# A two-block transformer kernel: expert weight loads moved and divided, residual products and a gather put elsewhere

## The chip, the cores and the metric

One core of a Trainium2 chip (trn2) runs the kernel. The metric is the device time of one execution in microseconds (us). Before the change, three runs took 1562.51, 1562.71 and 1564.31 us; the median is 1562.71. DMA rates are in GB/s, sizes of transfers in KB of the profile (2048 KB = 2.10 MB).

## The reference

Two blocks over 256 tokens of width 1024, float32 throughout. The second block ends in a mixer product and a mixture of experts, and only these two are touched:

```python
def second_block(x, ...):
    h = h + mixer_block(rmsnorm(h, norm1_g[l]), ...)   # ends in merged @ w_o
    h = h + hier_moe(rmsnorm(h, norm2_g[l]), w_group[l], w_router[l], w1[l], w3[l], w2[l])

def mixer_block(...):
    merged = sigmoid(gc) * y_conv + sigmoid(ga) * y_attn    # gc, ga = u @ w_in parts
    return merged @ w_o                                     # y_attn = attention @ w_attn_out

def hier_moe(u, ...):   # group by argmax, then the best 2 of its 8 experts
    # every expert e: (silu(x @ w1[e]) * (x @ w3[e])) @ w2[e], weighted, added to its tokens
```

There are 64 experts with an inner width of 512: w1, w3 and w2 are 2.10 MB each for an expert, 403 MB together, and each is read once from HBM.

## The kernel before, in words

**Engines and memory.** The five engines run programs written out by hand; semaphores order them. SyncE (SP) issues all weight loads, in one fixed order, each behind a wait for the semaphore which says that the place is free. While SP waits, everything behind it in that order waits too. The weights live in `arena`, 11 places of 2.10 MB (128 partitions x 4096 floats).

**The dense part.** Weight units ("wao0" is the first half of w_attn_out, "wo1" the second half of w_o) go through a ring of four places; TensorE adds 1 to `dense_used` for each unit that it is done with, and `static_units` waits for that count. The last four products are `seven(0)` to `seven(3)`, matrix products of 256 x 1024 x 1024 done as seven half-size products each with sums of operands made by VectorE (DVE), in the order 5, 1, 6, 7, 2, 3, 4 (line 1505); seven(2) is for ga, seven(3) for w_attn_out with the units wao0 and wao1. DVE reads these two units first for a difference of weights (line 2436). Then comes `wo(half, n)`, merged @ w_o for one half of the tokens (128) and one half of the columns (line 1557): eight matmuls 128x512 over the eight chunks of 128 rows. It reads the transposed merged rows from `mrg` (in arena place 8).

**Between the blocks' last product and the experts.** For each half of the tokens: DVE adds the product to `h_res` (line 2619), GpSimd (POOL) copies the result to `h` in another order of columns (line 793), ACT takes squares, TensorE turns h_res (`turn_h`, line 1565) and makes the router's product (`logits`, line 1577). DVE routes (lines 2632 to 2644), TensorE counts ranks (lines 1600, 1678, 1681 to 1683), DVE makes the selection matrix `sel` for the first two experts (line 2660). `gather_first(half)` (line 1618) multiplies h by sel: chunk c of 128 columns, 64 token places; ACT scales chunks 0 to 3 (line 3074), DVE chunks 4 to 7. Two products of the identity with the rows of the residual (lines 1679 and 1684 for token half 0, 1728 for half 1) put the residual into PSUM banks 0 to 3, to which every expert's result is added.

**The experts.** They are taken in 32 pairs. `MOE_SLOTS` numbers the places of arena; a pair has six units of 2.10 MB: k = 0 to 3 for w1 and w3, k = 4 and 5 for w2. Even pairs use one set of places, odd pairs another; place 0 serves both. Pair 0's w1 and w3 are loaded in quarters: arena places 0, 1 and 2 (`load_quarter`, lines 662 and 665; 4 x 512 KB and 4 x 1024 KB; they only wait for `attn2_done`, the end of the attention), then place 4. `first_up` (line 1700) is pair 0's up product: chunk by chunk c, four matmuls each; behind chunks 0, 1, 3 and 5 it adds 1 to `quarter_used`, by which SP loads pair 1's half pieces of place 0 (lines 729 and 731) and pair 2's first places (line 684). `first_rows` and `xg_ready` say that the gathered rows are there. All later pairs run `expert_up` (line 1630), `scatter` (1661), `gather_pair` (1610), `turn_pair` (1637, 1641), `expert_down` (1652). Place 5 (pair 0's k = 4) is free when half of pair 0's down product is done (`down_half`).

**Pair 1 before the change.** Its k = 1 goes to arena place 9 (free with wo0), k = 2 to place 10 (free with wo1), k = 4 to place 8 (mrg and others; free with wo1), k = 5 to place 3 (h_res and others; free when squares, POOL's copies and the residual products of token half 0 are done, `res_taken`). k = 4 and 5 are loaded in halves (`load_part`, line 715). The order on SP's queue is:

```python
for k in (0, 1, 2, 4, 5, 3) if pair in (1, 2) else range(UNITS_PAIR):
    if (pair, k) == (1, 1):
        load_part(4, 1)
        load_part(5, 0)
```

Of the kernel before, what the change touches and what calls it, by code (L numbers as in the profile page):

```python
# [233 lines left out]
def two_blocks(nc, t, out):  # L234

    with ExitStack() as ctx:
# [155 lines left out]
        mrg = xn2.rearrange("p a b -> p (a b)").rearrange("p (c s) -> p c s", c=KC)  # L392
# [63 lines left out]
        def moe_count(slot, turn):  # L456

            return 16 * turn + ((48 if turn == 1 else 64) if slot == 0 else 16 if slot in (1, 2, 3, 9, 10) else 0)
# [104 lines left out]
        quarter_used, res_taken = sem("quarter_used"), sem("res_taken")  # L563
# [56 lines left out]
        def _(sp):  # L620
# [32 lines left out]
            static_units(UNIT["downC"], len(UNITS))  # L653
# [33 lines left out]
            def moe_wait(pair, k):  # L687
# [24 lines left out]
            def load_part(k, part):  # L712

                at = moe_slot(1, k)
                sp.dma_start(MOE_SLOTS[at][:, part * 2048:(part + 1) * 2048], t["w2"][k - 2, :, part * 2048:(part + 1) * 2048]
                             ).then_inc(moe_loaded[at], 16)

            for pair in range(PAIRS):
                for k in (0, 1, 2, 4, 5, 3) if pair in (1, 2) else range(UNITS_PAIR):
                    if (pair, k) == (1, 1):  # L720
                        load_part(4, 1)
                        load_part(5, 0)
                    if pair == 1 and k in (4, 5):
                        moe_wait(pair, k)
                        load_part(k, k - 4)
                        continue
                    if (pair, k) == (1, 3):
# [3 lines left out]
                        sp.dma_start(MOE_SLOTS[0][:, 2048:4096], t["w3"][3, :, 2048:4096]).then_inc(moe_loaded[0], 16)  # L731
                        continue
# [68 lines left out]
        def _(pe):  # L801
# [745 lines left out]
            def wo(half, n):  # L1547
# [4 lines left out]
                for c in range(KC):  # L1552
                    if not n and c in (0, 4):
                        pe.wait_ge(mrg_ready, M_ORDER.index((half, c // 4)) + 1)
                    if not half and not n and c == 1:
                        release_seven(3)
                    last = mm(ps[:, BANKS[step][n], :], mrg[:, c, half * P:(half + 1) * P], slot_view(u)[:, c, :],  # L1557
                              start=(c == 0), stop=(c == KC - 1))
                last.then_inc(bank_filled, 1)
# [8 lines left out]
            def logits(half, n):  # L1568
# [7 lines left out]
                for c in range(4 * n, 4 * n + 4):  # L1576
# [20 lines left out]
            logits(1, 0)  # L1597
            turn_h(1, 1, (4, 3))
            pe.wait_ge(assigned, 1)
# [15 lines left out]
            def gather_first(half):  # L1615

                for c in range(KC):
# [4 lines left out]
                if half:  # L1622
# [1509 lines left out]
```

## Time and profile before

| | |
|---|---|
| median of 3 runs | 1562.71 us (1562.51 to 1564.31) |
| profiled execution | 1561.92 us, its span 1560.1 us |
| TensorE matmul busy | 1263.3 us (81% of the span) |
| DVE, ACT, POOL busy | 516.9, 228.8, 17.8 us |
| DMA | 501.40 MB, 321 GB/s over the span |
| chain that ended last | PE 58%, DMA 39%, DVE 1% |
| up products of the looped pairs (L1630) | 276.9 us busy, 255.4 us idle before, for DMA |

The span is cut into 40 slices of 39 us on the page: TensorE is full (9 tenths) in the first 19 and at 5 to 7 tenths in the rest; the DMA engines are at 9 tenths from about the same place on. Times of busy engines are not the kernel's time: what counts is which wait ends last in each stage. PE is TensorE, PEld its weight loads, SPq the queue of SyncE. A float32 matmul shows as two records. Lines (L1630) are those of the kernel before.

### The profile page before, as it was taken

The numbers are of one execution on the slowest core, as the hardware profiler recorded it, in microseconds if no ns is written. First come the engines' busy times: TensorE is split into PE (matmuls) and PEld (weight loads), VectorE is DVE, ScalarE is ACT, GpSimd is POOL, SyncE is SP. The second block draws the span as 40 slices with busy tenths as digits, with TensorE's granted clock in tenths as the row PEclk, the third lists the DMA queues.
The fourth block names the chain that finished last, engine by engine and source line by source line (L and its number), as shares of the span: only waits on it lengthen the run. The fifth ranks groups of instructions, "written<-read, shape, count | busy, mean of one in ns | idle before, by whom it ended". The sixth has DMA issues, their size and how long they took to land.

```text
span 1560.1 us, 16698 instructions
## 1 busy us (share of the span) xinstructions
PE 1263.3 (81%) x6953; PEld 642.1 (41%) x6953; DVE 516.9 (33%) x1096; ACT 228.8 (15%) x649; POOL 17.8 (1%) x30
## 2 busy tenths in 40 slices
PE   9999999999999999997676576577576576476577
PEld 4665644444588544543232232223233223223223
DVE  6554577785453674311011111111111111111101
ACT  2435213111122101211001001001001001001001
POOL 2000000000000000100000000000000000000000
PEclk9999999999999999999788888788888789788889
DMA  9531756405433449899999999999999999999997
GB/s 302 210 114 55 245 155 205 155 35 216 157 113 109 166 157 370 347 429 428 428 429 428 429 427 430 427 428 428 429 428 428 428 428 429 427 428 429 429 426 323
DMA packets 93419, 501.40 MB, mean 321 GB/s; under 512 B 6797, under 2 KB 34817, under 8 KB 68160
## 3 DMA queue, kind: packets, MB, share of 16 engines
q1 hardware_dynamic: 92608, 500.00, 78.9%
q0 software_dynamic: 768, 0.85, 0.3%
q8 instruction: 25, 0.41, 0.1%
q14 instruction: 18, 0.15, 0.0%
HBM read 499.78 MB, written 1.05 MB: 321 GB/s over the span
## 4 chain that ended last, share of the span: by engine, by line
PE 58%; DMA 39%; DVE 1%; issue 0%; SPq 0%; ACT 0%; DVEq 0%
DMA arena<-in_w 38%; PE ps L1630 17%; PE ps L1253 8%; PE ps L862 7%; PE ps L1505 6%; PE ps L1305 3%; PE ps L857 2%; PE ps L1067 2%; PE ps L1557 2%; PE ps L907 2%; PE ps L1437 2%; PE ps L1207 1%; DMA arena<-in_w_in 1%; PE ps L1375 1%; PE ps L1280 1%
## 5 line engine op out<-in xcount | busy, mean ns | idle before, releaser
L1630 PE MATMUL ps<-arena,hT 128*32 128x512 f32 x1984 | 276.9, 721 | 255.4 <-DMA arena<-in_w 255.4
L1630 PEld LDWEIGHTS ps<-arena,hT 128*32 128x32 f32 x1984 | 69.2, 130 | 462.6 <-issue 319.8
L2722 DVE TENSOR_TENSOR moe_hid<-moe_hid,ps 64x512 f32<-64x512 f32 x32 | 22.1, 690 | 482.8 <-ACT moe_hid L3090 482.8
L1652 PE MATMUL ps<-arena,moe_turned 128*32 128x512 f32 x1024 | 116.7, 595 | 28.0 <-DVE moe_turned L2724 27.8
L1610 PEld LDWEIGHTS ps<-sel,h 128*128 128x128 f32 x992 | 113.2, 192 | 24.1 <-issue 24.1
L1610 PE MATMUL ps<-sel,h 128*128 128x64 f32 x992 | 117.2, 276 | 0.0
L3090 ACT ACTIVATE moe_hid<-ps 64x512 f32<-64x512 f32 x32 | 18.8, 588 | 656.2 <-PE ps L1630 650.5
L862 PE MATMUL ps<-hT,arena 128*128 128x256 f32 x512 | 113.9, 380 | 0.1
L862 PEld LDWEIGHTS ps<-hT,arena 128*128 128x128 f32 x512 | 96.8, 190 | 15.0 <-issue 2.2
L3074 ACT ACTIVATE hT<-ps,gcol 128x64 f32<-128x64 f32 x252 | 55.0, 328 | 158.5 <-PE ps L1610 156.8
L1505 PE MATMUL ps<-arena 128*128 128x512 f32 x176 | 77.3, 593 | 0.0
L2724 DVE COPY moe_turned<-ps 128x512 f32<-128x512 f32 x32 | 22.1, 692 | 161.8 <-PE ps L1641 161.8
L1253 PE MATMUL ps<-arena 128*128 128x512 f32 x160 | 71.0, 592 | 0.0
L1652 PEld LDWEIGHTS ps<-arena,moe_turned 128*32 128x32 f32 x1024 | 32.7, 109 | 87.3 <-issue 70.6
L1661 PE MATMUL ps<-moe_y,moe_turned 64*128 64x512 f32 x256 | 63.6, 615 | 0.8 <-DVE moe_y L2726 0.8
L2726 DVE COPY moe_y<-ps 128x512 f32<-128x512 f32 x32 | 22.1, 691 | 123.4 <-PE ps L1652 123.4
L1253 PE MATMUL ps<-arena,hT 128*128 128x512 f32 x120 | 53.3, 592 | 0.0
L1505 PEld LDWEIGHTS ps<-arena 128*128 128x128 f32 x176 | 33.2, 190 | 41.1 <-issue 38.7
L1253 PEld LDWEIGHTS ps<-arena 128*128 128x128 f32 x160 | 29.8, 190 | 34.4 <-issue 34.2
L1305 PE MATMUL ps<-arena 128*128 128x512 f32 x96 | 42.6, 593 | 0.0
L1661 PEld LDWEIGHTS ps<-moe_y,moe_turned 64*128 64x128 f32 x256 | 22.0, 186 | 42.8 <-issue 41.1
L2177 DVE SCALAR_TENSOR_TENSOR arena<-ps,arena 128x255 f32<-128x255 f32 (+1 forms) x88 | 35.7, 472 | 6.9 <-ACT arena L2931 6.9
(465 smaller groups left out, 1245.4 us busy)
## 6 DMA issues: line engine op xcount, KB each, us to landing
arena<-in_w SPq DMA_DIRECT2D x184, 2048.0 KB, 29.3
arena<-in_w_in SPq DMA_DIRECT2D x18, 2048.0 KB, 8.5
arena<-in_w_up SPq DMA_DIRECT2D x22, 1024.0 KB, 9.4
arena<-in_w SPq DMA_DIRECT2D x14, 1024.0 KB, 13.2
arena<-in_w_down SPq DMA_DIRECT2D x5, 2048.0 KB, 13.7
arena<-in_w_out SPq DMA_DIRECT2D x2, 2048.0 KB, 14.3
arena<-in_w_conv_out SPq DMA_DIRECT2D x2, 2048.0 KB, 7.8
arena<-in_w_attn_out SPq DMA_DIRECT2D x2, 2048.0 KB, 7.8
```

Source lines behind the costliest of these rows:

```text
L857: last = mm(ps[:, at, :], xT[:, c, bank * P:(bank + 1) * P], w[:, c, :], start=(c == 0), stop=(c == KC - 1))
L862: last = mm(o, w[:, c, q * P:(q + 1) * P], xT[:, c, :], start=(c == 0), stop=(c == KC - 1))
L907: last = mm(ps[:, BANK1[product], :], lhs[:, c, :], rhs[:, c, :], start=(c == 0 and product != 3), stop=(c == 3), skip_group_check=True)
L1253: last = mm(up_seven_bank(m, product), lhs, rhs, start=(c == 0 and product not in (2, 3)), stop=(c == 3), skip_group_check=True)
L1305: return mm(ps[:, bank, :], x, w, start=(i == 0), stop=(i == NPAIR - 1))
L1505: last = mm(bank7(g, product), lhs, rhs, start=(c == 0 and product not in (2, 3)), stop=(c == 3), skip_group_check=True)
L1610: last = mm(ps[:, GT, c * 2 * CAP:(c + 1) * 2 * CAP], hview[:, half, c, :], sel[:, half, :], start=(half == 0), stop=(half == 1))
L1630: last = mm(ps[k * CAP:(k + 1) * CAP, UP, :], x[:, c, (k % 2) * CAP:(k % 2 + 1) * CAP], w[:, at:at + DE], start=(c == 0), stop=(c == KC - 1))
L1652: last = mm(ps[k * CAP:(k + 1) * CAP, DN, :], a[:, m * 64 + (k % 2) * CAP:m * 64 + (k % 2 + 1) * CAP], w[:, at:at + 512], start=(m == 0), ...
L1661: last = mm(ps[:, 2 * half + n, :], sT[rows, half * P:(half + 1) * P], moe_y[rows, :], start=False, stop=False, skip_group_check=True)
L2177: v.scalar_tensor_tensor(yy, u[:, 0:S - 2 + tap], prm[:, 0, c + 44 * tap:c + 44 * tap + 1], yy, ALU.mult, ALU.add).then_inc(ffn_chain if t ...
L3074: return a_(xg[:, c, :], ps[:, bank, c * 2 * CAP:(c + 1) * 2 * CAP], ACT.Copy, scale=gcol[:, 3, c:c + 1])
```

## The change

1. **Order of loads.** The eight quarter transfers into arena places 0, 1 and 2 are issued before wao0, wao1, wo0 and wo1 instead of behind them.
2. **Places given up in pieces.** The layout of `mrg` puts token half 0 into the first quarter of place 8's columns, token half 1 into the next; the first quarter is loaded (w2 of pair 1, k = 4, columns 0 to 1024) when wo(0, 1) is done, the second when wo(1, 1) is. wo(1, 1) adds 1 to `dense_used` behind its chunk 3, and the first half of place 10 is loaded then; the release at its end is one higher.
3. **Residual products.** All four (both token halves) stand behind first_up, before pair 1's gather, and read `h` (rows with a step of eight elements); `res_taken` is gone, and place 3 waits for `h_turned` instead.
4. **Router product.** logits(1, 0) is cut: chunks 0 and 1 before turn_h(1, 1), chunks 2 and 3 behind it.
5. **First gather.** Of token half 1, chunks 0 to 5 are gathered before first_up, chunks 6 and 7 between its chunks 1 and 2.

```diff
-        mrg = xn2.rearrange("p a b -> p (a b)").rearrange("p (c s) -> p c s", c=KC)
+        mrg = xn2.rearrange("p h (c s) -> p h c s", c=KC)
...
-            return 16 * turn + ((48 if turn == 1 else 64) if slot == 0 else 16 if slot in (1, 2, 3, 9, 10) else 0)
+            return 16 * turn + ((48 if turn == 1 else 64) if slot == 0 else 32 if slot == 9 else 16 if slot in (1, 2, 3, 8, 10) else 0)
...
-            static_units(UNIT["downC"], len(UNITS))
+            static_units(UNIT["downC"], UNIT["wao0"])
...
                     sp.wait_ge(rms_ready, 8)
                     sp.wait_ge(h_moved, 4)
-                    sp.wait_ge(res_taken, 1)
+                    sp.wait_ge(h_turned, 4)
                 else:
-                    sp.wait_ge(dense_used, released(UNIT[{3: "wao0", 4: "wao1", 7: "wo0", 8: "wo1", 9: "wo1"}[at]]))
+                    sp.wait_ge(dense_used, released(UNIT[{3: "wao0", 4: "wao1", 7: "wo0", 8: "wo1", 9: "wo1"}[at]]) + (at >= 8))
...
+            for k in range(3):
+                moe_wait(0, k)
+                load_quarter(MOE_SLOTS[k], k)
+            static_units(UNIT["wao0"], len(UNITS))
             for pair in range(PAIRS):
-                for k in (0, 1, 2, 4, 5, 3) if pair in (1, 2) else range(UNITS_PAIR):
+                for k in (0, 1, 2, 4, 5, 3) if pair in (1, 2) else range(0 if pair else 3, UNITS_PAIR):
                     if (pair, k) == (1, 1):
-                        load_part(4, 1)
-                        load_part(5, 0)
+                        load_part(4, 2048, 4096)
+                        load_part(5, 0, 2048)
+                        sp.wait_ge(bank_filled, filled(PROD["wo_h0"], 1))
+                        load_part(4, 0, 1024)
                     if pair == 1 and k in (4, 5):
                         moe_wait(pair, k)
-                        load_part(k, k - 4)
+                        load_part(k, *((1024, 2048), (2048, 4096))[k - 4])
                         continue
...
+                    if (pair, k) == (1, 2):
+                        at = moe_slot(1, 2)
+                        sp.wait_ge(dense_used, released(UNIT["wo1"]))
+                        sp.dma_start(MOE_SLOTS[at][:, 0:2048], t["w3"][2, :, 0:2048]).then_inc(moe_loaded[at], 16)
+                        moe_wait(1, 2)
+                        sp.dma_start(MOE_SLOTS[at][:, 2048:4096], t["w3"][2, :, 2048:4096]).then_inc(moe_loaded[at], 16)
                         continue
...
+                    if half and n and c == 3:
+                        last.then_inc(dense_used, 1)
...
-            logits(1, 0)
+            logits(1, 0, (0, 1))
             turn_h(1, 1, (4, 3))
+            logits(1, 0, (2, 3))
...
+            def take_residual(half, n):
+
+                rows = h[:, half, :].rearrange("p (c n) -> p n c", c=KC)[:, n * 64:(n + 1) * 64, :]
+                mm(ps[:, 2 * half + n, :], ident, rows, start=True, stop=False, skip_group_check=True)
...
-            mm(ps[:, 0, :], ident, h_res[:, 0, 0:512], start=True, stop=False, skip_group_check=True)
...
-            mm(ps[:, 1, :], ident, h_res[:, 0, 512:1024], start=True, stop=False, skip_group_check=True).then_inc(res_taken, 1)
             pe.wait_ge(sel_ready, 2)
             pe.wait_ge(h_moved, 4)
-            gather_first(1)
+            gather_first(1, range(0, 6))
             def first_up():
 
                 for c in range(KC):
+                    if c == 2:
+                        gather_first(1, (6, 7))
...
-                    for n in range(2):
-                        rows = h[:, 1, :].rearrange("p (c n) -> p n c", c=KC)[:, n * 64:(n + 1) * 64, :]
-                        mm(ps[:, 2 + n, :], ident, rows, start=True, stop=False, skip_group_check=True)
+                    for half in range(2):
+                        for n in range(2):
+                            take_residual(half, n)
```

How the instructions stand now. On SP's queue, before the dense part's last loads (in_w_attn_out_2 is wao, in_w_o_2 is wo, w1, w3 and w2 are expert weights; - is before, + is the change):

```order
 L633 DMA arena<-in_w_in_2 128x8x512 [waits dense_used] x2
-L633 DMA arena<-in_w_attn_out_2 128x8x512 [waits dense_used] x2
-L633 DMA arena<-in_w_o_2 128x8x512 [waits dense_used] x2
 L662 DMA arena<-in_w1_2 128x2x512 [waits attn2_done]
 L662 DMA arena<-in_w1_2 128x2x512
```

The four loads of wao and wo have moved down past the eight quarter transfers of places 0, 1 and 2, and now stand before those of place 4.

On the same queue, the loads of pair 1, from k = 0 to the first of pair 2:

```order
 L684 DMA arena<-in_w1_2 128x4096 [waits m_turned]
 L715 DMA arena<-in_w2_2 128x2048 x2
+L715 DMA arena<-in_w2_2 128x1024 [waits bank_filled]
 L684 DMA arena<-in_w1_2 128x4096 [waits dense_used]
-L684 DMA arena<-in_w3_2 128x4096 [waits dense_used]
-L715 DMA arena<-in_w2_2 128x2048 [waits dense_used]
-L715 DMA arena<-in_w2_2 128x2048 [waits res_taken,h_moved,rms_ready]
-L729 DMA arena<-in_w3_2 128x2048 [waits quarter_used]
-L731 DMA arena<-in_w3_2 128x2048 [waits quarter_used]
+L741 DMA arena<-in_w3_2 128x2048 [waits dense_used]
+L743 DMA arena<-in_w3_2 128x2048 [waits dense_used]
+L715 DMA arena<-in_w2_2 128x1024 [waits dense_used]
```

One transfer of 4096 columns has become two of 2048, and one of 2048 two of 1024, of which the first stands ahead of place 9's load; the rest keeps its order.

On TensorE, from the first token half's gather to first_up's third chunk, before:

```order
L1618 MATMUL ps<-sel,h 128x64 x7
L1678 MATMUL ps<-moe_turned,consts 128x64
L1679 MATMUL ps<-arena,consts 128x512
L1681 MATMUL ps<-moe_turned,consts 128x64 [waits assigned]
L1682 MATMUL ps<-moe_turned,consts 128x64
L1683 MATMUL ps<-moe_turned,consts 128x64
L1684 MATMUL ps<-arena,consts 128x512
L1618 MATMUL ps<-sel,h 128x64 [waits h_moved,sel_ready]
L1618 MATMUL ps<-sel,h 128x64 x7
L1700 MATMUL ps<-arena,hT 32x512 [waits moe_loaded0,first_rows]
```

and with the change, up to the two chunks inside first_up:

```order
L1698 MATMUL ps<-moe_turned,consts 128x64
L1700 MATMUL ps<-moe_turned,consts 128x64 [waits assigned]
L1701 MATMUL ps<-moe_turned,consts 128x64
L1702 MATMUL ps<-moe_turned,consts 128x64
L1638 MATMUL ps<-sel,h 128x64 [waits h_moved,sel_ready]
L1638 MATMUL ps<-sel,h 128x64 x5
L1720 MATMUL ps<-arena,hT 32x512 [waits moe_loaded0,first_rows]
L1720 MATMUL ps<-arena,hT 32x512 x3
L1720 MATMUL ps<-arena,hT 32x512 [waits first_rows]
L1720 MATMUL ps<-arena,hT 32x512 x3
L1638 MATMUL ps<-sel,h 128x64 x2
```

The two residual products (128x512) are gone from here, and two of the gather's eight matmuls stand behind eight of first_up's; a row further down, `L1728 MATMUL ps<-h,consts 128x512 x2` has become `L1633 MATMUL ps<-h,consts 128x512 x4`.

## Rows read from the trace of the kernel before

**Rows 1.** Page, parts 2 and 4: rate by slice, and the chain by line

```profile
GB/s 302 210 114 55 245 155 205 155 35 216 157 113 109 166 157 370 347 429 428 428 429 428 429 427 430 427 428 428 429 428 428 428 428 429 427 428 429 429 426 323
...
DMA arena<-in_w 38%; PE ps L1630 17%; PE ps L1253 8%; PE ps L862 7%; PE ps L1505 6%; PE ps L1305 3%; PE ps L857 2%; PE ps L1067 2%; PE ps L1557 2%; PE ps L907 2%; PE ps L1437 2%; PE ps L1207 1%; DMA arena<-in_w_in 1%; PE ps L1375 1%; PE ps L1280 1%
```

**Rows 2.** Chain of work, 540 to 700 us: start us, us, what

```profile
631.61 0.44 PE ps L1565 x4
...
641.85 6.88 PE ps L1557 x16
...
648.87 1.08 PE ps L1577 x8
...
656.10 0.91 PE ps L1684 x2
657.02 1.73 PE ps L1618 x16
658.75 7.00 PE ps L1700 x64
665.75 3.63 PE ps L1728 x4
...
685.10 12.72 DMA arena<-in_w
```

**Rows 3.** Windows: busy us (x) of PE, PEld, DVE, ACT, POOL, then PEclk, DMA share, GB/s

```profile
552.00:561.00 9.00, 9.00 (x22) 3.99 (x21) 8.48 (x10) 0.00 (x0) 0.00 (x0) 1.00 0.00 0
593.00:616.00 23.00, 23.00 (x61) 10.35 (x60) 12.68 (x14) 1.96 (x4) 0.00 (x0) 1.00 1.02 391
641.00:650.00 9.00, 8.85 (x34) 4.70 (x34) 3.36 (x15) 1.12 (x2) 0.49 (x1) 1.00 0.72 258
657.00:662.00 5.00, 5.00 (x49) 2.68 (x51) 2.60 (x13) 2.21 (x5) 0.00 (x0) 1.00 0.97 338
```

**Rows 4.** SP's queue, timeline 555 to 760 us: start, us, engine, line, operation

```profile
561.04 7.24 SPq L633 DMA_DIRECT2D arena<-in_w_attn_out  x2
...
592.36 3.40 SPq L662 DMA_DIRECT2D arena<-in_w  x4
```

**Rows 5.** Single transfers by line: issue duration ns, issue time, then us to landing

```profile
L633 SPq DMA_DIRECT2D arena<-in_w_in x1: 546/546/546, 543.9 to 543.9; - x1
...
DMA to landing us min/median/max: 7.9/7.9/7.9
...
L715 SPq DMA_DIRECT2D arena<-in_w x1: 328/328/328, 657.1 to 657.1; - x1
...
DMA to landing us min/median/max: 5.1/5.1/5.1
...
L729 SPq DMA_DIRECT2D arena<-in_w x1: 328/328/328, 659.8 to 659.8; - x1
...
DMA to landing us min/median/max: 5.8/5.8/5.8
...
L684 SPq DMA_DIRECT2D arena<-in_w x1: 328/328/328, 676.5 to 676.5; - x1
...
DMA to landing us min/median/max: 11.5/11.5/11.5
```

**Rows 6.** Timeline of DVE and PE, 579 to 590 us: DVE's sum for wao, PE's product

```profile
579.52 2.29 DVE L2436 TENSOR_TENSOR arena<-arena 128x2048 f32<-128x2048 f32 x1
...
584.79 3.60 PE L1505 MATMUL ps<-arena 128*128 128x512 f32 x8
```

**Rows 7.** Timeline, 631 to 662 us, in brackets idle time and releaser

```profile
649.51 1.09 POOL L793 COPY h<-arena 128x512 f32<-128x512 f32 x1 [8.72 <-DVE arena L2619]
...
655.22 0.43 PE L1681 MATMUL ps<-moe_turned,consts 128*128 128x64 f32 x2 [0.27 <-DVE moe_turned L2644]
...
656.59 2.02 PEld L1618 LDWEIGHTS ps<-sel,h 128*128 128x128 f32 x16 [0.41 <-DVE sel L2660]
...
657.89 0.93 ACT L3074 ACTIVATE hT<-ps,gcol 128x64 f32<-128x64 f32 x4 [1.78 <-PE ps L1618]
```

More of the change, by code:

```diff
@@ L562, in two_blocks @@
         piece_in = sem("piece_in")
-        quarter_used, res_taken = sem("quarter_used"), sem("res_taken")
+        quarter_used = sem("quarter_used")
         SEL_FIRST, SCATTERED_FIRST = PAIRS + 1, PAIRS + 1
@@ L706, in moe_wait, with load_part @@
                     sp.wait_ge(h_moved, 4)
[L707 removed]
+                    sp.wait_ge(h_turned, 4)
                 else:
[L709 to L712 removed]
+                    sp.wait_ge(dense_used, released(UNIT[{3: "wao0", 4: "wao1", 7: "wo0", 8: "wo1", 9: "wo1"}[at]]) + (at >= 8))
+            def load_part(k, lo, hi):
                 at = moe_slot(1, k)
[L715 to L716 removed]
+                sp.dma_start(MOE_SLOTS[at][:, lo:hi], t["w2"][k - 2, :, lo:hi]).then_inc(moe_loaded[at], 16)
+            for k in range(3):
+                moe_wait(0, k)
+                load_quarter(MOE_SLOTS[k], k)
+            static_units(UNIT["wao0"], len(UNITS))
             for pair in range(PAIRS):
[L719 removed]
+                for k in (0, 1, 2, 4, 5, 3) if pair in (1, 2) else range(0 if pair else 3, UNITS_PAIR):
                     if (pair, k) == (1, 1):
[L721 to L722 removed]
+                        load_part(4, 2048, 4096)
+                        load_part(5, 0, 2048)
+                        sp.wait_ge(bank_filled, filled(PROD["wo_h0"], 1))
+                        load_part(4, 0, 1024)
                     if pair == 1 and k in (4, 5):
                         moe_wait(pair, k)
[L725 removed]
+                        load_part(k, *((1024, 2048), (2048, 4096))[k - 4])
                         continue
@@ L1556, in wo @@
                         release_seven(3)
-                    last = mm(ps[:, BANKS[step][n], :], mrg[:, c, half * P:(half + 1) * P], slot_view(u)[:, c, :],
+                    last = mm(ps[:, BANKS[step][n], :], mrg[:, half, c, :], slot_view(u)[:, c, :],
                               start=(c == 0), stop=(c == KC - 1))
+                    if half and n and c == 3:
+                        last.then_inc(dense_used, 1)
                 last.then_inc(bank_filled, 1)
@@ L1566, in turn_h, with logits @@
                 last.then_inc(h_turned, 1)
-            def logits(half, n):
+            def logits(half, n, chunks=range(4)):
                 if n:
@@ L1575, in logits @@
                     pe.wait_ge(hT_act, 21 + half)
-                for c in range(4 * n, 4 * n + 4):
+                for c in (4 * n + k for k in chunks):
                     last = mm(ps[:, 6 - half, 0:NG + NE], hT[:, c, half * P:(half + 1) * P], router_w[:, c, :],
@@ L1612, in gather_pair, with gather_first @@
                 last.then_inc(gathered, 1)
-            def gather_first(half):
-                for c in range(KC):
+            def take_residual(half, n):
+                rows = h[:, half, :].rearrange("p (c n) -> p n c", c=KC)[:, n * 64:(n + 1) * 64, :]
+                mm(ps[:, 2 * half + n, :], ident, rows, start=True, stop=False, skip_group_check=True)
+            def gather_first(half, chunks=range(KC)):
+                for c in chunks:
                     last = mm(ps[:, 2 + c // 4, (c % 4) * 2 * CAP:(c % 4 + 1) * 2 * CAP], hview[:, half, c, :], sel[:, half, :],
@@ L1621, in gather_first @@
                         last.then_inc(first_rows, 1)
-                if half:
+                if half and KC - 1 in chunks:
                     last.then_inc(gathered, 1)
@@ L3043, in _ @@
                 act.wait_ge(m_turned, k + 1)
-                a_(mrg[:, 4 * n:4 * n + 4, half * P:(half + 1) * P], ps[:, bank, :].rearrange("p (c s) -> p c s", c=4),
+                a_(mrg[:, half, 4 * n:4 * n + 4, :], ps[:, bank, :].rearrange("p (c s) -> p c s", c=4),
                    ACT.Copy).then_inc(mrg_ready, 1)
```

1 line of the change is left out of this document (added).

## The prediction

> **What bounds the kernel now.** I read the page's second and fourth parts first. From slice 18 of 40 (39 us each, so from 663 us) the DMA rate stands at 426 to 430 GB/s up to the last slice, and 38% of the chain that ended last is "DMA arena<-in_w", the expert weights [rows 1]. The merged chain says where the ownership changes: up to 685.10 us it is made of TensorE work with short DVE pieces, at 685.10 TensorE waits 12.72 us for a weight transfer, and from there every pair of experts waits for its weights [rows 2]. The windows by stage show what the DMA engines did before that: nothing from 552 to 561, 391 GB/s from 593 to 616, then gaps again (258 GB/s from 641 to 650, 338 GB/s from 657 to 662) [rows 3], and from 662 the full rate of the page.
>
> So the end of the kernel is the moment at which the gapless stream begins, plus its bytes at 428 GB/s, plus a short tail. Work on TensorE counts only as far as it moves that moment, and transfers moved ahead count only if they leave fewer bytes for the time after it. Look at 640 to 662 us: by the rates there, 3.6 us of transfer time are lost in 641 to 650 ((428-258)/428 x 9) and 1.05 us in 657 to 662. What lies earlier was refilled: by 624 us everything issued so far has landed in both orders.
>
> **Transfers moved ahead of wao0.** Eight transfers, 6144 KB (6.29 MB), go from 592.4 us [rows 4] to right behind the issue at 543.9 us, into the empty 552 to 561. Worth by itself: nothing. The next loads (arena 4, 5, 6 and on) wait for TensorE, not for the queue, and they are issued at the same times as before. The price is on wao0 and wao1, issued at 561.0 and 567.9 [rows 4], now behind them. The last one before them lands at 543.9 + 7.9 = 551.8 [rows 5]; 6.29 MB and twice 2.10 MB at the 391 GB/s that such a mixture had [rows 3] take 26.8 us, so wao1 lands at 578.6. DVE first needs it at 579.52 and its next result is due for TensorE's matmuls at 584.79 [rows 6]; between the two lie 2.3 us for that sum and two adds of 0.7, so the slack is 0.9 us before DVE feels it, and about 2.5 us before TensorE does. Cost: 0, covered by that slack; if it were gone, each us late is a us on the end.
>
> **Places given up in pieces.** Behind wo(0, 1), whose successor starts at 631.61 [rows 2], a quarter of arena 8 (0.52 MB), at about 645.4 half of arena 10 (1.05 MB, when four of the eight matmuls of wo(1, 1), 6.88 us in all, are done), behind their end at 648.73 [rows 2] its rest and the other quarter of arena 8, and arena 3's half no longer behind the residual products (657.1 us [rows 5]) but behind the POOL copy that ends at 649.51 + 1.09 = 650.6 [rows 7]. From about 641.5 us on, 0.52 + 2.10 + 1.05 + 1.05 + 0.52 + 1.05 = 6.29 MB are then queued with hardly a gap: 14.7 us at 428 GB/s, done near 656.5. That fills the hole of 641 to 650, but opens one behind it: the next transfer, half of arena 0, waits for the first chunk of first_up. The gain therefore is only how much sooner that transfer runs.
>
> **TensorE up to first_up.** (a) Half of logits(1, 0) moves behind turn_h(1, 1), which waits for an add on DVE: four records of 0.135 us (1.08/8 [rows 2]) leave the front, and some 0.35 us of them stay in front of logits(1, 1), which waits for DVE's copy anyway. I take 0.2 us gained. (b) The residual product at 656.10 (0.91 us [rows 2]) and its twin go. But the weight load of the second gather half, at 656.59, waited for DVE's sel [rows 7]; the matmuls behind it began when the array was free, 657.02. With the array empty they begin right behind the first load: 656.72 (one load takes 2.02/16 = 0.13), so 0.3 us gained, not 0.9 or 1.8. (c) Chunks 6 and 7 of the gather's second half, 4 of 16 records in 1.73 us, are 0.43 us less before first_up. first_up also needs ACT's first chunk: copies begin right behind chunk 3 (657.89 [rows 7]), now at 657.4, and the first ends 0.33 later. So first_up starts near 657.9 instead of 658.75: **0.8 us** earlier, and the half of arena 0 is issued at 659.0 instead of 659.8.
> Before, that transfer took 5.8 us, because the queue was still busy; the 1.05 MB issued at 657.1 took 5.1 [rows 5]. It lands at 659.0 + 5.1 = 664.1 instead of 665.6: 1.5 us.
>
> **Pair 0 behind it.** The two gathered chunks come back between chunks 1 and 2 (0.43 us), so the rest of first_up ends only 0.4 us earlier. Then four residual products instead of two: 4 records take 3.63 us [rows 2], 0.91 each, twice the 0.455 of the removed ones, as they read h with a step of eight elements; so +3.63 us. All later steps of pair 0 and pair 1 up to 697.8 come 3.6 - 0.4 = 3.2 us later, and so do the releases of arena 5 and 6: the load of arena 5, issued at 676.5, goes to 679.7. Before, it took 11.5 us (landing 688.0 [rows 5]), since it queued. With the stream 1.5 us ahead it would land at 686.5, but a 2.10 MB transfer that starts alone needs 5.1 + 1.05/0.428 = 7.5 us: 687.2. So 0.7 to 1.5 us are left; I take **1.0 us**. The next issue, 685.1 going to 688.3, still has two transfers (10 us) queued ahead of it, and pair 1 ends before the stream's next landing or 1 to 2 us behind it, under a backlog of over 5 us. Nothing further is lost.
>
> The mrg layout changes no instruction count: 0 us. The three longer SP rows (142 against 145 in the order) are issue slots of 0.33 to 0.8 us while SP waits: 0.
>
> **Sum.** The profiled execution took 1561.92 us (span 1560.1), 0.79 below the median of the three runs, 1562.71. 1562.7 - 1.0 = **1561.7 us** for the median. About 0.2% (3.1 us) is what a measurement can tell from no change, so this is "the same".
>
> **Rivals.**
> 1. *All removed TensorE work lies on the path.* 0.9 + 0.9 + 0.43 us and the 0.2: first_up 2.4 us earlier, and with 0.7 us for the queue the stream is 3.1 us ahead; arena 5's release is then only 1.2 us later and hidden. 1559.6 us. For it: the chain names the residual product. Against: the DVE wait of the weight load, and the wait for DVE before 655.22 [rows 7] that swallows the first one. Chance 0.12.
> 2. *wao1 comes too late (slower).* If the stream of 552 to 578 runs at 340 GB/s or less instead of 391, wao1 lands at 582.7 or later; beyond 581.1 TensorE's product of seven(2) waits and everything behind moves one for one: 1562.7 - 1.0 + 1.6 = 1563.3 at 340 GB/s, 1567 at 300. Against it: 391 GB/s was measured for this mixture. Chance 0.09, half of it over 3.1 us.
> 3. *The longer pair 0 eats the gain.* If first_up starts where it did, the loads of arena 5 land at 676.5 + 4.1 + 7.5 = 688.1: no gain, 1562.8 us; with another us of late issue, 1564. Chance 0.10.
> 4. *Pieces pay a fixed price.* A 1 MB transfer alone takes 5.1 us for 2.45 us of bytes. Two transfers are added between 625 and 657; at 2.7 us each the early queue ends at 661.9, and the half of arena 0 lands near 667.0: 1562.7 + 1.4 = 1564.1. Against it: in the rows the transfers of 0.5 and 1 MB ran back to back at 391 GB/s without such a price. Chance 0.03.
> The Trainium skill, DMA: Bandwidth & Descriptors, section Rules for kernel authors, asks for at least 1 MiB per DMA for full bandwidth, and its section Bandwidth gives 6.15 us for 1 MB alone; by that rule the two quarters of arena 8 would be the dear ones and rival 4 the outcome. The rows of this case speak against it as long as the queue is filled.
>
> **How the numbers follow.** Forecast 0.66 (1560.9 to 1562.5 with the run-to-run spread of 1 us), rivals 0.12, 0.09, 0.10, 0.03. The range 1559.3 to 1564.0 takes in rivals 1, 3 and the small form of 2, and leaves out the large form of 2 and part of 4. Faster by over 0.2%: most of rival 1's upper half, 0.10. Slower by over 0.2%: 0.06. Same: 0.84.
>
> **What the changed profile would show.** Right: no empty window at 552 to 561 and an emptier one near 603 to 611; DVE's sum still at 579.5; over 420 GB/s from 641 to 656 and a hole of 3 to 4 us at 657 to 661; the half of arena 0 issued at 659.0 and landing at 664.1; arena 5's load issued at 679.7, landing at 686.5 to 687.2; TensorE's first long DMA wait ending near 697. Wrong: seven(3) or seven(2) waiting on DVE or DMA; first_up starting before 657 or after 658.5; a DMA hole near 680 to 683 longer than 1 us.

## The result, and the profile after

| | before | after |
|---|---|---|
| median | 1563.34 us (15 runs, 1562.22 to 1567.14) | 1567.19 us (15 runs, 1565.43 to 1569.89) |
| profiled execution | 1561.92 us, span 1560.1 | 1566.28 us, span 1564.5 |
| TensorE matmul busy | 1263.3 us | 1269.7 us |
| DMA | 501.40 MB | 501.40 MB |

The ratio after/before is 1.0023, 95% interval 1.0016 to 1.0031: **the change makes the kernel about 3.6 us slower** by this ratio (the medians lie 3.9 us apart). Forecast were 1561.7 us and no change, with a range up to 1564.0.

On the page of the changed kernel (the rows for [rows 1]) nothing seems to have happened: the same gapless stream, the same owners of the chain. TensorE is busy for 6.4 us more, though the change gives it only about 1.8 us of additional work by the rows of before (four strided products for two strided and two plain ones).

```profile
GB/s 301 211 113 54 248 155 200 160 29 215 161 108 114 172 306 214 346 397 429 428 429 429 429 428 429 428 428 428 429 428 429 428 428 429 429 428 428 428 427 321
...
DMA arena<-in_w 37%; PE ps L1650 17%; PE ps L1265 8%; PE ps L874 7%; PE ps L1517 6%; PE ps L1317 3%; PE ps L869 2%; PE ps L1079 2%; PE ps L1569 2%; PE ps L919 2%; PE ps L1449 2%; PE ps L1219 1%; DMA arena<-in_w_in 1%; PE ps L1387 1%; PE ps L1720 1%; PE ps L1292 1%
```

Slice 18, the first of the stream, has 397 GB/s instead of 429. So the loss lies at the stream's start. The windows of the changed kernel (columns as in [rows 3]: busy us of PE, PEld, DVE, ACT, POOL, then PEclk, DMA share, GB/s) show it:

```profile
552.00:561.00 9.00, 9.00 (x23) 3.99 (x22) 8.48 (x10) 0.00 (x0) 0.00 (x0) 1.00 1.04 398
593.00:616.00 23.00, 23.00 (x60) 10.40 (x59) 12.69 (x14) 2.15 (x4) 0.00 (x0) 1.00 0.49 178
641.00:650.00 9.00, 8.85 (x33) 4.57 (x33) 3.36 (x15) 0.93 (x2) 0.30 (x1) 1.00 0.99 375
657.00:662.00 5.00, 5.00 (x28) 2.66 (x27) 0.65 (x6) 2.21 (x5) 0.00 (x0) 0.52 0.31 129
662.00:685.00 23.00, 22.22 (x138) 9.45 (x138) 4.42 (x15) 2.33 (x9) 0.00 (x0) 0.96 0.97 375
```

The first three rows are as intended: the empty window is full, the later one emptier, and the hole of 641 to 650 gone (375 for 258 GB/s). The fourth has what no step of the prediction had: PEclk 0.52, where [rows 3] has 1.00. TensorE runs there at the lower of its two clocks, 1.2 GHz for 2.4, and the DMA hole in the same window is 3.5 us long ((428-129)/428 x 5). From 662 to 685, with 428 GB/s before, another 2.8 us of transfer are lost ((428-375)/428 x 23).

The chain of work of the changed kernel, for [rows 2]:

```profile
655.39 0.45 PE ps L1700 x2
...
656.76 2.49 PE ps L1638 x12
659.25 3.57 PE ps L1720 x16
662.82 1.05 PE ps L1638 x4
663.87 5.35 PE ps L1720 x48
669.22 7.11 PE ps L1633 x8
...
710.00 11.53 DMA arena<-in_w
```

Twelve records of the gather (L1638) take 2.49 us, 0.21 each; before, sixteen took 1.73, 0.11 each [rows 2]. first_up's first sixteen records (L1720) take 3.57 us, 0.22 each, its last 48 are back at 0.11. So the low clock holds over nearly all of the gather, the first two chunks and the two chunks inside first_up. TensorE's first long wait for weights begins at 710.0 and ends at 721.5; before it began at 685.1 [rows 2], and the forecast had it end near 697. It comes a pair later.

What TensorE did before the clock fell, from the timeline (in brackets idle time and releaser):

```profile
655.39 0.44 PE L1700 MATMUL ps<-moe_turned,consts 128*128 128x64 f32 x2 [1.17 <-DVE moe_turned L2664]
...
656.76 2.49 PE L1638 MATMUL ps<-sel,h 128*128 128x64 f32 x12 [0.49 <-DVE sel L2680]
```

Where before a residual product ran and 0.27 us was left idle [rows 7], 1.17 us are idle; where the second one ran, 0.49 us. Three releases that decide the stream, as single transfers by line (issue duration ns, issue time, then us to landing), for [rows 5]: the half of place 3, the first half of place 0, the load of place 5:

```profile
L715 SPq DMA_DIRECT2D arena<-in_w x1: 328/328/328, 650.9 to 650.9; - x1
...
DMA to landing us min/median/max: 9.3/9.3/9.3
...
L734 SPq DMA_DIRECT2D arena<-in_w x1: 328/328/328, 661.2 to 661.2; - x1
...
DMA to landing us min/median/max: 5.2/5.2/5.2
...
L684 SPq DMA_DIRECT2D arena<-in_w x1: 328/328/328, 683.5 to 683.5; - x1
...
DMA to landing us min/median/max: 8.1/8.1/8.1
```

The first half of place 0 lands at 666.4 (before 665.6), its second half, which waits for a chunk more at the low clock, at 670.2 (before 668.1), place 5 at 691.6 (before 688.0). From 742 us to the last weights every landing is 4.1 to 4.5 us later than in the trace of before, and the profiled execution ends 4.4 us later. The stream is the bound, and what is lost is lost at its start.

### The profile page after: what moved, and what is told of

It reads as the page before. It is cut to its first block, busy times and chain, and to the rows that moved or that the text cites. A ratio compares the mean times of both kernels' runs of the same rounds, so it can differ in the third digit from the quotient of the medians.

```text
span 1564.5 us, 16700 instructions
## 1 busy us (share of the span) xinstructions
PE 1269.7 (81%) x6953; PEld 645.8 (41%) x6953; DVE 517.0 (33%) x1096; ACT 228.8 (15%) x649; POOL 18.1 (1%) x30
## 2 busy tenths in 40 slices
DMA packets 93707, 501.40 MB, mean 320 GB/s; under 512 B 6829, under 2 KB 34849, under 8 KB 68448
## 4 chain that ended last, share of the span: by engine, by line
PE 59%; DMA 38%; DVE 1%; SPq 0%; issue 0%; ACT 0%; DVEq 0%
DMA arena<-in_w 37%; PE ps L1650 17%; PE ps L1265 8%; PE ps L874 7%; PE ps L1517 6%; PE ps L1317 3%; PE ps L869 2%; PE ps L1079 2%; PE ps L1569 2%; PE ps L919 2%; PE ps L1449 2%; PE ps L1219 1%; DMA arena<-in_w_in 1%; PE ps L1387 1%; PE ps L1720 1%; PE ps L1292 1%
## 5 line engine op out<-in xcount | busy, mean ns | idle before, releaser
L3110 ACT ACTIVATE moe_hid<-ps 64x512 f32<-64x512 f32 x32 | 18.8, 588 | 656.5 <-PE ps L1650 647.8
```

## The experiments

Two theories. **Clock**: without the residual products TensorE has gaps behind which it is granted 1.2 GHz, and first_up comes late. A filler below is a product whose result nothing uses and which only keeps TensorE at work. **Pair 0**: the four strided products at its end release place 5 too late. Each run is compared with the unchanged kernel on the same chip (35 runs in each set; medians 1563.8 for the first four kernels, 1563.25 for the next four, 1562.65 for the last four). The ratio comes with its 95% interval, about 0.1% to either side, and is not exactly that of the medians. "Stream" is how much later than in the trace of before the transfers land from 742 us on (the median over them). It compares two single executions, and they are not level when they reach the place in question: DVE's first routing step (line 2632) starts at 652.15 in the trace of before and 0.1 to 0.5 us later in the others (3.3 in experiment 5, 1.8 in 6, see the end). So the last few tenths of a stream number are not the edit's.

**1. Filler products in both gaps.**

```diff
+            mm(ps[:, 0, 0:N_KEPT], ident, consts[:], start=True, stop=True)
             pe.wait_ge(assigned, 2)
...
+            mm(ps[:, 1, 0:N_KEPT], ident, consts[:], start=True, stop=True)
             pe.wait_ge(sel_ready, 2)
```

> The changed kernel with two matmuls of the identity and constants (480 columns, into banks 0 and 1) where the two residual products stood. Theory A (clock): with them gone TensorE idles before 655.4 and before 656.8, the granted clock falls to half at 657.2 for 6.8 us, and the second gather and the first chunks of first_up run at half speed. With the fillers the clock stays full, first_up's first chunk is done near 659, the half of place 0 lands near 664.5 and the time is 1562 to 1563.5 us, 4 us under the change. Theory B (longer pair 0): the loss is the four strided residual products, which are still there, so the time stays at 1567. Theory C (order and pieces of the loads): stays at 1567 too.

Measured: 1564.93 us, ratio 1.0010 (1.0000 to 1.0021). Windows, chain and the transfer into place 5 of this kernel:

```profile
657.00:662.00 5.00, 5.00 (x45) 2.65 (x47) 1.62 (x11) 2.21 (x5) 0.00 (x0) 1.00 0.57 184
662.00:685.00 23.00, 22.21 (x150) 9.10 (x146) 5.96 (x21) 2.33 (x9) 0.00 (x0) 1.00 0.98 402
```

```profile
656.29 0.86 PE ps L1704 x2
657.15 1.28 PE ps L1638 x12
658.43 1.88 PE ps L1722 x16
```

```profile
L684 SPq DMA_DIRECT2D arena<-in_w x1: 328/328/328, 680.4 to 680.4; - x1
...
DMA to landing us min/median/max: 9.2/9.2/9.2
```

More work on TensorE, and the clock stays at 1.00: the gather takes 1.28 us instead of 2.49, first_up starts 0.8 us earlier in spite of the filler. The transfer ahead of place 5 lands 1.2 us earlier than before (the forecast of the change had 1.5), place 5's 1.6 us later: that load took 9.2 us, though the one ahead of it had landed 1.5 us after its issue. The stream is 1.0 us behind. The time lies above the 1562 to 1563.5 that theory A gave and below theory B's 1567, so both hold a part.

**2. The residual products of token half 0 back in their places**, the rest of the change kept.

```diff
+            mm(ps[:, 0, :], ident, h_res[:, 0, 0:512], start=True, stop=False, skip_group_check=True)
             pe.wait_ge(assigned, 2)
...
+            mm(ps[:, 1, :], ident, h_res[:, 0, 512:1024], start=True, stop=False, skip_group_check=True).then_inc(res_taken, 1)
             pe.wait_ge(sel_ready, 2)
```

> The changed kernel with the residual products of token half 0 back at their two places (from h_res, res_taken again), the other parts of the change kept. Theories A and B both give 1561 to 1562.5 us (clock full, pair 0 not longer, stream 1 to 1.5 us ahead of the kernel before). Theory C keeps 1566 to 1567.

Measured: 1564.57 us, 1.0008 (0.9997 to 1.0019); clock 1.00, stream 0.7 us behind. Most of the loss is gone, but the stream is not 1 to 1.5 us ahead and the time not 1561 to 1562.5, as expected.

**3. No residual of token half 0 at all**, on the changed kernel: the gaps stay, pair 0 is not longer. The result lacks that residual.

```diff
-                    for half in range(2):
-                        for n in range(2):
-                            take_residual(half, n)
+                    for n in range(2):
+                        take_residual(1, n)
```

> The changed kernel without any residual products for token half 0: the residual of tokens 0 to 127 is left out of the result. Theory A: the clock still falls at about 657; place 5 is released 3.6 us earlier than in the change (near 679.9 instead of 683.5), so its load queues behind the stream again and the stream is only as late as its start: 1564 to 1565.5 us. Theory B: all of the loss is gone, 1562 to 1563. If the clock alone were the loss, 1567 stays.

Measured: 1566.29 us, 1.0013 (1.0003 to 1.0023). The first half of place 0 is issued at 661.7, clock 0.50 in the window 657 to 662, stream 2.7 us behind; place 5's load lands 4.9 us behind the one ahead of it, as before. The gaps alone cost, a little more than the 1564 to 1565.5 expected.

**4. The kernel before with part 3 of the change only** (place 3 waits for `h_turned`, as in the change).

```diff
-            mm(ps[:, 0, :], ident, h_res[:, 0, 0:512], ...)
...
-            mm(ps[:, 1, :], ident, h_res[:, 0, 512:1024], ...).then_inc(res_taken, 1)
...
+                    for half in range(2):
                         for n in range(2):
```

> The kernel before with only the residual products moved behind first_up. Theory A with B: clock at half for 6.8 us from about 657, place 5 released 7 us later, 1567 to 1569 us. Theory C: 1563 as before.

Measured: 1567.50 us, 1.0020 (1.0009 to 1.0031), stream 4.6 us behind: the whole loss of the change. Its window and its chain:

```profile
657.00:662.00 5.00, 4.90 (x24) 3.89 (x28) 2.04 (x13) 2.21 (x5) 0.00 (x0) 0.50 0.78 328
```

```profile
657.10 3.67 PE ps L1618 x16
660.77 8.40 PE ps L1698 x64
```

The gather of 1.73 us and the up product of 7.00 [rows 2] take 3.67 and 8.40.

**5. Filler in the first gap only** (the first of the two products of 1).

```diff
+            mm(ps[:, 0, 0:N_KEPT], ident, consts[:], start=True, stop=True)
             pe.wait_ge(assigned, 2)
```

> The changed kernel with one matmul of 480 columns of constants at the first place only (before the wait for assigned, where TensorE idles 1.2 us), none at the second. If the length of idle time around 654 to 657 decides on the clock, most of it is filled and the clock stays full: stream as with both fillers, 1564 to 1565 us. If the second, shorter idle time (0.5 us) decides, the clock falls as in the change: 1567.

Measured: 1564.37 us, 1.0004 (0.9994 to 1.0014). Filling the first gap takes away most of the loss; filling only the second (12) does not. But the clock did not stay full in the profiled execution, the slowest of the ten (1568.25 us), in which everything is some 3.2 us later from 95 us on:

```profile
662.00:670.00 8.00, 8.00 (x64) 2.60 (x60) 3.04 (x13) 1.28 (x1) 0.00 (x0) 0.80 0.76 246
```

It fell at 661.8 for 3.4 us, inside first_up, instead of 6.8 us from within the gather. What the other nine did isn't known.

**6. The kernel before with the load order only.**

```diff
+            for k in range(3):
+                moe_wait(0, k)
+                load_quarter(MOE_SLOTS[k], k)
+            static_units(UNIT["wao0"], len(UNITS))
```

> The kernel before with only the eight quarter transfers issued ahead of wao0. My theory (nothing by itself, since the next loads wait for TensorE): 1563 to 1564.3, the same as before; wao1 lands at 578.4 as in the change and no wait appears in seven(2). Rival: the later wao or the emptier queue before 616 costs something, 1565 or more.

Measured: 1563.04 us, 0.9999 (0.9988 to 1.0010). Nothing, as forecast. In its trace wao1 landed at 581.2, 11.6 us behind its issue (10.3 in the change), and DVE's sum waited 0.2 us for it; TensorE did not.

**7. The kernel before with the pieces only.**

```diff
+                        sp.wait_ge(bank_filled, filled(PROD["wo_h0"], 1))
+                        load_part(4, 0, 1024)
...
+                    if half and n and c == 3:
+                        last.then_inc(dense_used, 1)
```

> The kernel before with only the places given up in pieces (mrg layout, two halves of place 10, two quarters of place 8). Theory: the early bytes end sooner but the stream starts at the same issue (659.8), so 0 to 0.5 us better than before, no difference that can be measured. Rival (fixed price of a piece): 1 us or more slower, with the half of place 0 landing at 667.

Measured: 1563.35 us, 1.0003 (0.9993 to 1.0013). Two windows of it:

```profile
641.00:650.00 9.00, 8.85 (x34) 4.70 (x34) 3.36 (x15) 1.00 (x2) 0.38 (x1) 1.00 1.01 386
657.00:662.00 5.00, 5.00 (x49) 2.79 (x51) 2.65 (x14) 2.21 (x5) 0.00 (x0) 1.00 0.76 256
```

The hole moves from 641-650 to 657-662, and the half of place 0 is issued at 659.9 and lands at 665.6, as before [rows 5]. No price for smaller pieces either: the stream stays within 0.3 us of before. The Trainium skill, DMA: Bandwidth & Descriptors, section Rules for kernel authors, asks for at least 1 MiB per DMA; here two pieces of 0.52 MB, issued into a filled queue, cost nothing that shows.

**8. A version made to fit**: the changed kernel, but the residual of token half 0 is taken inside the two gaps from `h_res`, 768 columns in the first and 256 in the second, so that neither wait is left idle, the gather isn't delayed, and pair 0 isn't longer.

```diff
+            mm(ps[:, 0, :], ident, h_res[:, 0, 0:512], start=True, stop=False, skip_group_check=True)
+            mm(ps[:, 1, 0:256], ident, h_res[:, 0, 512:768], start=True, stop=False, skip_group_check=True)
             pe.wait_ge(assigned, 2)
...
+            mm(ps[:, 1, 256:512], ident, h_res[:, 0, 768:1024], start=False, stop=False, skip_group_check=True).then_inc(res_taken, 1)
             pe.wait_ge(sel_ready, 2)
```

> The changed kernel, but the residual of token half 0 is taken from h_res inside TensorE's two waits: 512 and 256 columns before the wait for assigned (1.4 us of work for a wait of 1.5), the last 256 columns before the wait for sel (0.46 us for 0.63); pair 0 is not longer. Theory: clock full, the second gather starts with sel at 656.8 instead of 657.4, the half of place 0 is issued near 659.2, place 5's load keeps its queue; stream 0.5 to 1 us ahead of the variant with the residual products back at their old places: 0 to 1 us better than the kernel before, 1563 to 1564 beside 1563.8. If 256 columns are too little to hold the clock it falls at 657 and the time is 1565 to 1566.

Measured: 1562.90 us, 1.0000 (0.9991 to 1.0008). Its chain:

```profile
656.22 0.49 PE ps L1705 x2
...
656.71 1.55 PE ps L1638 x12
658.27 1.88 PE ps L1723 x16
```

The gather begins 0.3 us earlier than before, first_up 0.5, place 5's load lands at 687.6 (before 688.0), and the stream is 0.3 us ahead. That is all that the other four parts give here, and a measurement doesn't tell it from nothing.

**9. The kernel before without its residual products of token half 0** (nothing added; the result lacks that residual; place 3 waits for `h_turned`, as in 4).

```diff
-            mm(ps[:, 0, :], ident, h_res[:, 0, 0:512], ...)
...
-            mm(ps[:, 1, :], ident, h_res[:, 0, 512:1024], ...).then_inc(res_taken, 1)
```

> The kernel before without the two residual products of token half 0 anywhere (the residual of tokens 0 to 127 is left out of the result): the idle time alone, pair 0 no longer than before. Theory: the clock falls at about 657 and the gather and the first two or three chunks of first_up run at half; the half of place 0 is issued near 661.5 to 662.7 and the stream starts some 2 us late, 1565 to 1566 beside 1563.3 to 1563.8. If the products' own time counted, it would be 1561.5 to 1563.

Measured: 1566.72 us, 1.0020 (1.0010 to 1.0031): a kernel with 1.8 us less TensorE work is slower. Windows and chain:

```profile
655.00:657.00 2.00, 1.47 (x6) 1.28 (x6) 1.27 (x8) 0.77 (x5) 0.00 (x0) 0.64 0.93 393
657.00:662.00 5.00, 4.97 (x24) 3.89 (x28) 2.14 (x13) 2.21 (x5) 0.00 (x0) 0.50 0.73 306
```

```profile
657.02 3.67 PE ps L1618 x16
660.70 9.55 PE ps L1698 x64
670.25 3.63 PE ps L1726 x4
```

The gather starts at the same 657.02 as before [rows 2], in spite of the two products left out. The products run at half the clock for 10.2 us from 655.6. The stream is 3.9 us behind, all of it already at the transfer ahead of place 5. A second stretch at the low clock, 3.4 us from 679.5, hits pair 0's down product and costs the stream nothing that shows. The rest of the 5.6 us by which this execution ends later is at its end (see 10).

**10. The kernel before with pair 0 longer only** (the strided products done twice, same result).

```diff
-                    for n in range(2):
+                    for n in (0, 1, 0, 1):
```

> The kernel before with its two strided residual products done twice (same result): four of them behind first_up, everything ahead of them as before, clock full. Place 5's load is issued at 676.5 + 3.6 = 680.1. If a load into a queue that still holds 1 to 3 us of work loses nothing, the stream is at most 0.5 us later: 1563.5 to 1564. If it loses what the variant with fillers showed (landing 9.2 us behind the issue), place 5 lands near 689.3 instead of 688.0: 1 to 1.5 us later, 1564.5 to 1565.

Measured: 1565.33 us, 1.0014 (1.0005 to 1.0023). Windows and the transfer into place 5:

```profile
657.00:662.00 5.00, 5.00 (x46) 2.88 (x48) 2.92 (x16) 2.21 (x5) 0.00 (x0) 1.00 0.97 342
662.00:685.00 23.00, 22.22 (x150) 9.12 (x146) 4.87 (x15) 2.34 (x9) 0.00 (x0) 1.00 0.99 413
```

```profile
L684 SPq DMA_DIRECT2D arena<-in_w x1: 328/328/328, 680.4 to 680.4; - x1
...
DMA to landing us min/median/max: 8.2/8.2/8.2
```

With the full clock there are 413 instead of 428 GB/s between 662 and 685, and the load lands 5.4 us behind the one ahead of it instead of 4.9. So the second mechanism exists by itself, but in this trace it is worth 0.5 us, below the 1 to 1.5 expected. The stream is 1.5 us behind: four later transfers, up to 719 us, took 5.0 to 5.6 us each instead of 4.9, for no reason that the trace names. The rest of the 3.1 us by which this execution ends later is at its end, where the last down product ran at a low clock. Its rows in the trace of before and in this one, and the window of this one:

```profile
1548.66 3.98 PE L1652 MATMUL ps<-arena,moe_turned 128*32 128x512 f32 x32 [0.78 <-DVE moe_turned L2724]
...
1550.06 5.34 PE L1652 MATMUL ps<-arena,moe_turned 128*32 128x512 f32 x32 [0.78 <-DVE moe_turned L2724]
```

```profile
1550.00:1555.00 5.00, 4.94 (x32) 1.27 (x32) 0.01 (x1) 0.00 (x0) 0.00 (x0) 0.66 0.06 24
```

The traces of 9 and 11 have the same fall of the clock near 1552 us, for 3.4 us; behind the last weights' landing these three take 10.3 to 10.5 us, all others 8.6 to 9.1. The longer pair 0 is not its cause, for 9 and 11 have none.

**11. The kernel before with parts 4 and 5 only.**

```diff
-            logits(1, 0)
+            logits(1, 0, (0, 1))
             turn_h(1, 1, (4, 3))
+            logits(1, 0, (2, 3))
...
-            gather_first(1)
+            gather_first(1, range(0, 6))
...
+                    if c == 2:
+                        gather_first(1, (6, 7))
```

> The kernel before with only the router product and the first gather divided. The products of the residual stay where they are, so the clock stays full. From the variant with them put back: 0.4 us of the gather come back earlier, the split of logits gives nothing since ACT's copy of the turned rows ends at the same time. The half of place 0 is issued at 659.4 to 659.8: 1562.8 to 1563.8, the same.

Measured: 1564.38 us, 1.0006 (0.9995 to 1.0016), above the 1562.8 to 1563.8 expected; its profiled execution has the slow end of 10. first_up starts at 658.5 (before 658.75). logits(1, 1) starts at 651.2, where before it starts at 650.95, no more apart than the two traces are anyway: ACT's copy, which ends there, comes behind ACT's squares and not behind the moved product, so part 4 gives nothing.

**12. Filler in the second gap only.**

```diff
+            mm(ps[:, 1, 0:N_KEPT], ident, consts[:], start=True, stop=True)
             pe.wait_ge(sel_ready, 2)
```

> The changed kernel with one matmul of 480 columns only at the second place (before the wait for sel). With the filler at the first place alone the profiled execution still had half clock for 3.4 us, from 661.8, in first_up. If it is the sum of work over these microseconds that decides, this one should behave alike: the clock falls in some executions, median 1564 to 1566, between 1564.9 with both fillers and 1567.2 with none.

Measured: 1568.03 us, 1.0029 (1.0017 to 1.0040), the highest ratio of all and above the 1564 to 1566 expected. Its timeline and chain:

```profile
655.49 0.69 PE L1700 MATMUL ps<-moe_turned,consts 128*128 128x64 f32 x2 [1.17 <-DVE moe_turned L2665]
```

```profile
657.03 1.71 PE ps L1703 x2
658.74 2.45 PE ps L1638 x12
```

Behind the first gap the products are slow already (0.69 us for 0.45), the filler itself takes 1.71 us for 0.86, and the gather starts 2.0 us later than in the changed kernel. The clock fell at 655.3 here, ahead of the filler, so in this execution the filler only added its time at the low clock. Up to the filler the program is that of the change, where the clock fell at 657.2: when it falls varies from one execution to the next.

**All profiles together.** The five kernels with both gaps or with only the second filled (the change, 3, 4, 9, 12) have the clock at 0.50 in the window 657 to 662 (0.52 in the change). The eight that keep a product in both gaps (before, 1, 2, 6, 7, 8, 10, 11) have 1.00. In 5, with the first gap filled, it fell later and for half as long.

## Why the prediction was wrong

- **What bounds the kernel**: right. The end is the stream's start plus its bytes. In the change a landing late by 4.1 us at 742 is late by 4.3 at 1550. In the other traces what is late at 742 is still late at 1550, less up to 0.7 us (1.1 in 12, 1.4 in 5). Behind the last weights the traces of 9, 10 and 11 take 1.7 to 1.9 us more than before, where the forecast had only a short tail (experiment 10).
- **Transfers moved ahead, at 0**: right (experiment 6). wao1 landed at 578.4 (forecast 578.6), and DVE's sum started at 579.7. Rival 2 did not come, though in the trace of experiment 6 its slack on DVE was used up.
- **Pieces, hole filled and moved**: right (375 GB/s at 641 to 650; a hole behind 657; place 3's half issued at 650.9, forecast 650.6), but done at 660.2, not 656.5. Worth nothing by itself, and no fixed price (experiment 7): rival 4 falls.
- **TensorE up to first_up: this step failed.** Its (b) priced the two removed products as time only, 0.3 us gained, and the sum had no term for the clock. The gaps that they leave (1.17 and 0.49 us for 0.27 and less) are followed by 1.2 GHz. At full clock the step would have come out: 656.76 + 1.28 (experiment 1's gather) = 658.0 against 657.9 forecast, and the half of place 0 1.1 us behind it, at 659.1 against 659.0. It was issued at 661.2: 2.1 us late through the clock, and landed 5.2 us later as forecast (5.1). (b)'s own reading was right: the gather started at 656.76, forecast 656.72. (a), the divided router product, gave 0 instead of 0.2 us.
- **Pair 0: mechanism right, price too small.** The four products take 7.11 us (forecast 3.63 more; measured 3.48 more). The Trainium skill, SBUF — State Buffer, section Door 1: The DMA port swizzle, says that accesses which leave a 16-byte line each time pay a penalty; the trace agrees (0.455 us per record for the plain read, 0.89 for the strided one). But the load issued when the queue held only 1.5 us of work took 9.2 us (experiment 1), not the 7.5 worked out from a 1 MB transfer: at full clock place 5 landed 1.6 us late where 1.0 early was forecast. In the change it took 8.1 us. With the clock, first_up's end (669.22 for 665.75) and the products shift place 5's issue by 7.0 us, to 683.5 for 679.7 forecast.
- **"Nothing further is lost"**: nearly right. In the change one more transfer, landing at 706.7, took 5.4 us instead of 4.9.
- **Rival 3** (longer pair 0) named the second half of it and held it at 1564 at most, without the first half.

How the parts share the loss, by the ratios: the gaps alone +0.20% (experiment 9) and +0.13% (3), pair 0 alone +0.14% (10), both together +0.20% (4) and +0.23% (the change). With 0.1% to either side of each this does not say whether they add. The traces say more. How many us later than before each lands:

| | transfer ahead of place 5 | place 5 | stream | end of the execution |
|---|---|---|---|---|
| the change | 1.8 | 3.6 | 4.3 | 4.4 |
| 4, part 3 only | 3.1 | 4.8 | 4.6 | 4.5 |
| 3, gaps only | 3.0 | 3.0 | 2.7 | 3.0 |
| 9, gaps only | 4.1 | 4.1 | 3.9 | 5.6 |
| 1, gaps filled | -1.2 | 1.6 | 1.0 | 0.8 |
| 10, pair 0 longer only | 0.1 | 0.6 | 1.5 | 3.1 |
| 8, made to fit | -0.4 | -0.4 | -0.3 | 0.2 |

In the change 1.8 us are lost ahead of place 5, where 1.2 us were gained at full clock (1); place 5's late load adds 1.8, and the transfer at 706.7 half a us. Where the clock fell earlier (655.6 in 9, 656.8 in 4, 656.7 in 3, 657.2 in the change), more is lost ahead of place 5. Parts 1, 2, 4 and 5 show nothing: ratios of 0.9999 to 1.0006 (6, 7, 11, and 8 with all of them), of which the highest has an interval up to 1.0016.

In experiments 2 and 11 the first half of place 0 landed 7.0 and 6.7 us behind its issue instead of 5.8, and 0.4 and 0.2 us were missing already at 652 us; that is their 0.7 to 0.8 us. Open: why that transfer was slower, why place 5's load varies as it does, and how much of experiment 10's +0.14% is pair 0, since its profiled execution has 0.5 us of it at place 5's load and the rest elsewhere.

## What to carry to other kernels

A small product that fills a wait may be what keeps TensorE at 2.4 GHz: before it is removed, look at the idle time that it leaves and at what critical work follows. Put such work where the engine would wait anyway, and cut it to the wait's size (experiment 8), instead of moving it behind a busy stretch from which a transfer's release depends. And where transfers bound the end, price each release by how much of the queue is left when it comes, not by the engine time it costs.

## What was not expected of the hardware

- **Short gaps were enough here.** 1.17 us of idle time behind a stretch of small products was followed by 1.2 GHz at once in experiment 12 (0.69 us for 0.45), and in the change only behind the second gap, of 0.49 us (0.45, then 2.49 for twelve records). The Trainium skill, TensorE: Matmul & The Clock Gate, section Why this matters for your kernels, warns of idle gaps between bursts of matmuls, longer ones than these. Here the measurement decides: the gaps that cost were 1.2 and 0.5 us, and that row of the page gives no warning of them. It may not happen in each run: two of the twelve runs of experiment 12 took 1562.45 and 1562.94 us, but they were not profiled.
- **The clock falls at other places too, in some executions.** The unchanged kernel's runs lie in groups near 1562.3, 1563.9 and 1566.8 us. The profiles of experiments 5 and 6, whose program is the old one there, show the clock low near 95 us, in the dense part:

```profile
94.00:98.00 4.00, 4.00 (x32) 3.06 (x32) 3.10 (x13) 0.95 (x3) 0.00 (x0) 0.65 0.00 0
98.00:102.00 4.00, 4.00 (x14) 3.04 (x12) 3.24 (x11) 1.80 (x8) 0.00 (x0) 0.50 1.02 318
```

```profile
94.00:98.00 4.00, 4.00 (x26) 2.90 (x25) 2.67 (x9) 0.90 (x2) 0.00 (x0) 0.57 0.00 0
```

  In 5 (first fence) it is low for 6.8 us and everything behind is 3.2 us later, in 6 for 3.4 us and 1.6 us later. Behind the fall near the end in 9, 10 and 11 the time after the last weights is 1.7 to 1.9 us longer than before. That the groups of before come from such falls is possible, but was not tested; the one profile of before shows neither.
- **A nearly empty queue was dear.** Place 5's load of 2.10 MB lands 4.9 us behind its predecessor where the queue is full (before: issued 6.6 us ahead of the predecessor's landing). Issued 1.4 to 2.8 us ahead of it, it landed 5.4 (experiment 10), 6.6 (4), 6.7 (the change), 7.7 (1) and 8.1 us (5 and 12) behind it: 0.5 to 3.2 us lost, though bytes were still under way in each case. Why it varies so much is open.
